# Branch rows converted by thirds of tokens as soon as their readers are done, branch projection steps given out by stage

## What is computed

```python
h = _rmsnorm(x, norm_in_w)
u = h @ w_in                       # z | x,B,C | dt | q,k,v x 3 | z_att | q_mem | z_mem | merge gates
y_ssd, new_conv, new_ssm = _ssd_branch(z_ssd, xbc, dt_raw, ...)      # conv, chunked scan, gated norm
y_att = o_att * silu(z_att);  y_mem = mem_attn(q_mem, mem_kv) * silu(z_mem)
merged = gates[0] * (y_ssd @ w_br_ssd) + gates[1] * (y_att @ w_br_att) + gates[2] * (y_mem @ w_br_mem)
y = _rmsnorm(x + merged @ w_out, norm_f_w)
```

## Time and profile before

| | us |
|---|---|
| median of 3 runs | 2108.25 (2104.48 to 2114.3) |
| the profiled execution | 2112.42 |
| its span on the core | 2110.6 |
| PE busy | 1979.0 (94%) |
| DVE, ACT, POOL busy | 985.8, 765.1, 242.0 |
| mean granted clock of TensorE | 0.965 of full |

### The profile page before, as it was taken

One profiled execution on the slowest core, in us unless ns is written; L12 is line 12 of the kernel. 1 busy time (PEld: TensorE's weight loads), 2 busy tenths in 40 slices (PEclk: granted clock), 3 DMA queues, 4 the chain that ended last, 5 costly groups with the idle time before them and its releaser, 6 DMA issues.

```text
span 2110.6 us, 34859 instructions
## 1 busy us (share of the span) xinstructions
PE 1979.0 (94%) x14301; PEld 1892.0 (90%) x14301; DVE 985.8 (47%) x1941; ACT 765.1 (36%) x1642; POOL 242.0 (11%) x358
## 2 busy tenths in 40 slices
PE   5999999999989999999999899999999669969997
PEld 5899999999989999999999889669999659969997
DVE  5303676535465354443337684013555455454523
ACT  5223444323353333332655223115556532133202
POOL 1000111100001010112212100001211111100000
PEclk9999999999999999999999999998999879989999
DMA  6311332311112121212256784764545635554422
GB/s 216 92 42 52 93 93 83 93 46 40 49 33 65 41 67 39 87 44 90 86 170 198 237 260 141 268 228 134 169 153 161 216 88 179 175 173 140 143 84 104
DMA packets 171742, 257.18 MB, mean 122 GB/s; under 512 B 20229, under 2 KB 115269, under 8 KB 171557
## 3 DMA queue, kind: packets, MB, share of 16 engines
q1 hardware_dynamic: 149328, 187.97, 28.4%
q0 software_dynamic: 22256, 66.98, 9.4%
HBM read 188.13 MB, written 66.76 MB: 121 GB/s over the span
## 4 chain that ended last, share of the span: by engine, by line
PE 85%; DVE 5%; ACT 4%; DMA 3%; issue 2%; SPq 0%; POOL 0%; DVEq 0%; ACTq 0%; POOLq 0%
PE bank L2296 21%; PE bank L2297 21%; PE bank L2298 21%; PE bank L2496 3%; PE bank L2469 2%; PE bank L2452 2%; PE bank L2711 2%; PE bank L2600 1%; PE bank L2430 1%; DVE w_lo L1762 1%; PE bank L2755 1%; PE bank L2533 1%; DMA sums<-sum_T 1%; PE bank L2395 1%; PE bank L2394 1%
## 5 line engine op out<-in xcount | busy, mean ns | idle before, releaser
L2296 PE MATMUL bank<-w_hi,hT_hi 128*128 128x256 f32 (+1 forms) x1848 | 536.9, 291 | 0.2 <-issue 0.2
L2297 PE MATMUL bank<-w_lo,hT_hi 128*128 128x256 f32 (+1 forms) x1848 | 524.6, 284 | 0.0
L2298 PE MATMUL bank<-w_hi,hT_lo 128*128 128x256 f32 (+1 forms) x1848 | 523.6, 283 | 0.0
L2296 PE MATMUL bank<-hT_hi,w_hi 128*128 128x352 f32 x1344 | 451.3, 336 | 6.3 <-DVE acc L2143 5.7
L2298 PE MATMUL bank<-hT_hi,w_lo 128*128 128x352 f32 x1344 | 439.1, 327 | 0.0
L2297 PE MATMUL bank<-hT_lo,w_hi 128*128 128x352 f32 x1344 | 438.8, 327 | 0.0
L2296 PEld LDWEIGHTS bank<-w_hi,hT_hi 128*128 128x128 f32 (+1 forms) x1848 | 349.8, 189 | 1.9 <-issue 0.5
L2298 PEld LDWEIGHTS bank<-w_hi,hT_lo 128*128 128x128 f32 (+1 forms) x1848 | 350.6, 190 | 0.6
L2297 PEld LDWEIGHTS bank<-w_lo,hT_hi 128*128 128x128 f32 (+1 forms) x1848 | 349.7, 189 | 1.3
L2296 PEld LDWEIGHTS bank<-hT_hi,w_hi 128*128 128x128 f32 x1344 | 257.8, 192 | 20.1 <-issue 8.6
L2297 PEld LDWEIGHTS bank<-hT_lo,w_hi 128*128 128x128 f32 x1344 | 258.8, 193 | 0.5
(11 more groups left out here) (423 smaller groups left out, 2934.6 us busy)
## 6 DMA issues: line engine op xcount, KB each, us to landing
w_raw<-in_w_in SPq DMA_DIRECT2D x96, 512.0 KB, 5.0
kvring<-in_cache_win_kv SPq DMA_DIRECT2D x98, 256.0 KB, 4.8
feat_T<-fstage POOLq DMA_DIRECT2D x40, 528.0 KB, 4.2
fstage<-feat_T SPq DMA_DIRECT2D x16, 528.0 KB, 4.2
xc<-feat_T SPq DMA_DIRECT2D x8, 1024.0 KB, 5.9
sums<-sum_T SPq DMA_DIRECT2D x32, 256.0 KB, 4.5
o_rows<-obuf POOLq DMA_DIRECT2D x48, 132.0 KB, 2.0
mo<-o_rows SPq DMA_DIRECT2D x24, 264.0 KB, 3.3
```

The costliest lines, as they stand in the source:

```text
L2296: pe.matmul(out, xh(k), wh(k), start=(k == 0), stop=False)
L2297: pe.matmul(out, xh(k), wl(k), start=False, stop=False)
L2298: ins = pe.matmul(out, xl(k), wh(k), start=False, stop=(k == nk - 1))
```

## The change

What it does, in the order of the kernel:
- Rows are no longer converted whole. Item g = 0 to 8 of `ya` and `yb` is third g // 3 of the tokens of rows 0 to 2, 3 to 5 or 6 and 7 (`YA_ROWS`): one load of 3 (2) runs of 352, one instruction on ACT, one on DVE. The loads have steps of their own, `yal` as before and `ybl` new.
- The last gate chunk's groups are dealt so that both readers of the first third come first, and `ya` 0 to 5 run between the gate groups, each as soon as its third has been read (`gates_read`). `ya` 6 to 8 follow the last gate group; ("p1", 52, 0, 0, 0) stands among them.
- `p1` groups wait for their third and branch alone (`s_yal` of 2 to 8).
- The scan's last steps are dealt in stages: 18 `p1` groups over the last ten groups of the prompt's scan, 4 over the next six, 10 over the 26 sample groups, 4 over the last five; 12 follow. Before it was one for each.
- `yb` overwrites the memory of `ya` (`hT`) by thirds behind the last `p1` groups that read it; `p2`'s result takes the memory that `yb` had. `yb` has a fourth buffer, `acc0`. `normf`, `osq` lie elsewhere.
- ("split", n) and ("low", n) keep their place at the end of their chunk; of the last gate chunk and of the last `p1` chunk they stand where the lists below show them.

```diff
+YA_ROWS = (slice(0, 3), slice(3, 6), slice(6, 8))
+YA_SLOT = (0, 1, 2, 0, 1, 2, 0, 1, 0)
+YB_SLOT = (0, 1, 2, 0, 3, 1, 2, 0, 3)
+P1_SCAN, P1_STATE, P1_SAMPLE, P1_LAST = 18, 4, 10, 4
...
-    n_gate, n_ya = 31, 4
-    core[n_gate - 3] += [("yal", k) for k in range(3)]
-    for i in range(n_ya):
-        core[n_gate + i] += [("yal", k) for k in ((3, 4), (5, 6), (7,), ())[i]]
-        core[n_gate + i] += [("ya", 2 * i), ("ya", 2 * i + 1)]
-    sched += spread(core[:n_gate], gate_steps(len(fill_src)))
-    for x in core[n_gate:n_gate + n_ya]:
-        sched += x
+    n_gate = 5 * (NB - 2) + 1
...
+    f00, f01, f02, f10, f11, f12 = [x[:1] for x in steps[-6:]]
+    steps[-6:] = [f00, f10, f01, f02, f11, f12 + [("split", last_gate)]]
+    sched += spread(core[:n_gate], steps)
...
-        steps.append([("split", n)])
-    sched += spread(core[n_gate + n_ya:], steps)
+        if i < 3:
+            steps[-1].append(("split", n))
+    parts = [(core[n_gate:n_gate + 1], 0), (core[n_gate + 1:n_gate + 11], P1_SCAN), (core[n_gate + 11:n_gate + 17], P1_STATE)]
+    parts += [(core[n_gate + 17:n_gate + 43], P1_SAMPLE), (core[n_gate + 43:], P1_LAST)]
+    done = 0
+    for groups, k in parts:
+        sched += spread(groups, steps[done:done + k])
+        done += k
+    sched += [("ssd", NB, 6)] + [("ybl", g) for g in range(3)]
+    for step in steps[done:-6]:
+        sched += step
+    b00, b01, b02, b10, b11, b12 = steps[-6:]
+    sched += b00 + [("yb", 0), ("ybl", 3), ("ybl", 4)] + b01 + b10 + [("yb", 1), ("ybl", 5), ("yb", 2), ("ybl", 6)]
+    sched += b02 + [("yb", 3), ("ybl", 7)] + b11 + [("yb", 4), ("ybl", 8), ("yb", 5), ("yb", 6)] + b12 + [("yb", 7), ("yb", 8), ("split", n)]
+    g = last_gate
+    behind(("ssd", NB - 4, 4), 0, [("yal", k) for k in range(3)])
+    behind(("feat", g, 1, 0), 0, [("ya", 0)])
+    behind(("ssd", NB - 4, 6), 0, [("ya", 1), ("yal", 3)])
+    behind(("ssd", NB - 3, 4), 0, [("ya", 2), ("yal", 4), ("yal", 5)])
+    behind(("feat", g, 1, 1), 0, [("ya", 3), ("ya", 4)])
+    behind(("feat", g, 1, 2), 0, [("yal", 6), ("ya", 5)])
+    behind(("ssd", NB - 2, 1), 0, [("p1g", 0, 0), ("yal", 7), ("ya", 6), ("p1g", 0, 1)])
+    behind(("ssd", NB - 2, 2), 0, [("ya", 7), ("yal", 8)])
+    behind(("p1", g + 1, 0, 0, 0), 0, [("ya", 8), ("low", g)])
...
                 elif s[0] == "ya":
-                    k = s[1]
-                    if k == 0:
-                        act.wait_ge(s_pj, n_act_proj)
-                    act.wait_ge(s_kv[k % 3], kv_loads(k % 3) + 16 * (k // 3 + 1))
-                    act.activation(yAh[:, k, :], ya_slot(k), ACT.Copy).then_inc(s_yah, 1)
+                    g = s[1]
+                    act.wait_ge(s_pj, gates_read[g // 3])
+                    act.wait_ge(s_kv[YA_SLOT[g]], kv_loads(YA_SLOT[g]) + ya_loads(YA_SLOT[g], g + 1))
+                    act.activation(ya_part(yAh, g), ya_slot(g), ACT.Copy).then_inc(s_yah, 1)
...
-                    if s[0] == "p1" and u == n_act_proj:
-                        pe.wait_ge(s_yal, KT8)
-                    if s[0] == "p2" and s[2:] == (0, 0) and chunks[n][1] == 0:
-                        pe.wait_ge(s_yal, KT8 + KT8)
+                    if s[0] == "p1" and u < n_act_proj + 6:
+                        pe.wait_ge(s_yal, 3 * s[4] + 2 + s[3])
+                    if s[0] == "p2" and chunks[n][1] + s[2] == 0:
+                        pe.wait_ge(s_yal, N_YA + 3 * s[3] + 3)
```

More of the change, by code:

```diff
@@ L975, in snew, with ya_slot, ya_part, ya_loads @@
             return (Lflat[:, D:2 * D] if b % 2 == 0 else yo[:, :]).rearrange("p (i n) -> p i n", i=8)
-        def ya_slot(k):
-            return (yraw, acc1, acc0)[k % 3][:, :]
+        def ya_slot(g):
+            rows = YA_ROWS[g % 3]
+            return (yraw, acc1, acc0)[YA_SLOT[g]][:, 0:THIRD * (rows.stop - rows.start)].rearrange("p (k n) -> p k n", n=THIRD)
+        def ya_part(buf, g):
+            j = g // 3
+            return buf[:, YA_ROWS[g % 3], THIRD * j:THIRD * j + THIRD]
+        def ya_loads(at, g):
+            return 16 * sum(YA_SLOT[x] == at for x in range(g))
+        def ya_last(at, g):
+            return 1 + max(x for x in range(g) if YA_SLOT[x] == at)
+        gates_read = [1 + max(u for x, u in proj.items() if x[0] == "feat" and x[3] == j) for j in range(3)]
         def acc_of(ft):
@@ L991, in build_program, with yb_slot, yb_sem, yb_landed @@
             gate_no["p2", ft] = n_sig
-        def yb_slot(k):
-            return (yraw2, gate2, acc2)[k % 3][:, :]
+        def yb_slot(g):
+            rows = YA_ROWS[g % 3]
+            return (yraw2, gate2, acc2, acc0)[YB_SLOT[g]][:, 0:THIRD * (rows.stop - rows.start)].rearrange("p (k n) -> p k n", n=THIRD)
+        def yb_sem(at):
+            return s_kv[(0, 1, 2, 5)[at]]
+        def yb_landed(g):
+            at = YB_SLOT[g]
+            x = (0, 1, 2, 5)[at]
+            return yb_sem(at), kv_loads(x) + (ya_loads(at, N_YA) if at < 3 else 0) + 16 * sum(YB_SLOT[i] == at for i in range(g + 1))
+        def yb_done(at, upto):
+            return N_YA + 1 + max(i for i in range(upto) if YB_SLOT[i] == at)
+        last_p1 = chunks.index(next(x for x in chunks if x[0] == "p1" and x[1] == KT8 - 2))
+        def rows_read(g):
+            return proj["p1", last_p1, 1, int(g % 3 > 0), g // 3] + 1
         def yst_of(c):
@@ L1182, in _ @@
                     load_gate(ft, br)
-                elif s[0] == "yb":
-                    k = s[1]
-                    if k == 0:
+                elif s[0] == "ybl":
+                    g = s[1]
+                    at, j, rows = YB_SLOT[g], g // 3, YA_ROWS[g % 3]
+                    if g == 0:
                         last_free(sp)
```

84 lines of the change are left out of this document (46 added, 38 removed).

## The result

The changed kernel took 2124.72 us (median of 6 runs, 2119.67 to 2128.77) against 2108.42 us beside it: a ratio of 1.0079, 95% interval 1.0060 to 1.0097. It is slower by 16 us, outside the range given. Its profiled execution took 2119.67 us for a span of 2117.8, 7.2 us above the span of before; the same kernel, run again later, took 2117.40 us (10 runs, ratio 1.0041, 1.0022 to 1.0060), and that profiled execution had a span of 2122.8. I use both. Neither profile is of a middle execution: the first is of the fastest of its six (2119.67 us), the second of the slowest of its ten (2124.54), and the profile of before is of an execution of 2112.42 us, 4 us above the median of its set and 5 to 6 above those of the later ones. Executions of over 3000 us (one of e7_ask_fill22, one of e12_fill22, and one of before in each of two sets) are left out of all medians.

What follows compares the result with a forecast made beforehand. The prediction took PE's idle time, from order on ACT, DVE and SP, as the bound; its terms went from 55.5 to 54.6 us, 1 us less, giving 2107 us (own range 2098 to 2116; 8 in 10 within 2092 to 2120).

Steps and rivals of the forecast that it cites:

- What bounds the kernel now: Opening step, 1660.3 to 1899.3 us: PE's work is unchanged, so only its idle time, 55.5 us, is summed.
- Rival (b): TensorE's clock: if the 14 us freed at 1700 us leave it fast, some 8 us more come back, 2099 us; chance 0.12.
- Rival (c): Slower: weights asked for behind the conversions land as late as 12.6 us, 11.5 us more, 2118 us; chance 0.18.
- Rival (a): Transfers land near their floor, 10.5 us less, 2096 us; chance 0.20.
- up to the last gate: Conversions ahead of the weight split and chunk 5's state on DVE: PE's idle time 0 to about 1 us.
- products of chunk 6: PE's wait before scan chunk 6's masked decay products, for chunk 53's late weights: 12.4 to 12.5 us.
- state of chunk 6: PE's wait before the second half of chunk 6's state, no conversion left ahead on DVE: 16.9 + 0.9 to 3.8 us.
- chunk 7: Scan chunk 7: chunk 52's split steps now stand ahead of its state, and a third group awaits a bank: 6.4 to 11.9 us.
- sample tokens: Sample steps: fewer groups between them (1.8 to 3.5 us) and chunk 53's weight split (5 us): 1.8 to 8.5 us.
- end: Last projections and p2: waits for banks 4.0, split 2.6, gate 4.5, conversions 1.3, p2 3.9 us; in all 17.1 to 16.9.
- sign of being right: Waits before Lm over 10 us, chunk 6's state near 4, chunk 7's near 10, sample part about 5; PE stops in p2.
- three signs of being wrong: Chunk 7's state wait below 6 us; idle time over 60 us; a p1 eviction waiting long for its gate.

Runs made afterwards that it cites:

- e7_ask_fill22: Changed kernel with weights of chunks 53 to 57 asked for early and projection groups dealt 10, 2, 22, 2; 2105.78 us, ratio to before 0.9981.
- e12_fill22: Changed kernel, conversions and requests as they are, with projection groups dealt 10, 2, 22, 2 (22 among the sample steps); 2106.26 us, ratio to before 0.9999.
- e9: Kernel before with only the dealing by stage, 10 projection groups and one split over the 26 groups of sample steps; 2115.43 us, ratio 1.0041.
- e4: Changed kernel with one gate row asked for ahead of the first three reads of merged rows; 2112.74 us, ratio to before 1.0034.
- e1: Changed kernel with weights of chunks 53 to 57 asked for right behind the low part of the chunk before; 2104.14 us, ratio to before 0.9996.
- e3: Changed kernel with split and low of chunk 52 behind the second part of scan chunk 7, not ahead; 2125.43 us, ratio to before 1.0094.
- e11: Kernel before with weights of chunks 53 to 57 asked for right behind the low part of the chunk before; 2105.91 us, ratio 1.0004.
- e10_combined: Changed kernel with early weights, groups dealt 12, 4, 16, 4, and one gate row ahead of the first merged rows; 2100.02 us, ratio to before 0.9969.

## Why the prediction was wrong

**The step that failed** is the one under "What bounds the kernel now": "the work of PE is the same before and after ... The sum is one of idle time." The work is the same, with 14301 matmuls in both; its clock is not. The sum has no term for it. The sample part's term went over "fewer groups now lie between the sample steps" and charged only the cover that they gave (1.8 us made 3.5). What those groups also did was to hold the clock; their absence costs 7 us in one profile of the changed kernel and 12 in the other, 9 in e9, and that comes back in e12. The forecast of 2107 us was 18 us low against the first set of runs and 10 against the second; in their profiles the idle sum is 2.7 and 1.2 us above the forecast, and the clock takes 7 and 12 us more than before.

**Rival (b)** named the clock but with one sign: freed time gives clock back, "against it, the new waits of 10 and 5 us slow it elsewhere". The loss needed no waits (e9). Nor did clock come back at chunk 6: from 1600 to 1750 us PE lost 8.7 us to it before and 10.3 and 9.2 in the two profiles of the changed kernel. The rows read for it were the mean of the whole stretch, 0.84, and one window at a wait. In the same 239 us the changed kernel has

```profile
1660.30:1899.30 239.00, 187.41 (x1130) 178.43 (x1129) 111.95 (x207) 61.38 (x110) 24.78 (x25) 0.81 0.46 147
```

with PE busy for 4 us more and the clock at 0.81. A row for the sample part alone, and the count of projection groups in it, were what the prediction lacked.

**Rival (c)**, 2118 us, is near the result by its number, and its mechanism did not happen. It needed landings of 12 us. On SP and ACT of the changed kernel:

```profile
1722.76 0.53 SPq L1173 DMA_DIRECT2D w_raw<-in_w_br_mem  x1
```

```profile
1729.46 1.91 ACT L1507 ACTIVATE w_hi<-w_raw 128x2048 fp32r<-128x2048 f32 x1 [14.13 <-DMA w_raw<-in_w_br_mem]
```

the weights of chunk 54 landed 6.7 us after the second request; 7.9 and 7.6 us for chunks 53 and 55. **Rival (a)**, landings at the floor of 4.8 us, did not happen either. The forecast had 7 us for chunk 54, with an estimate of 6.1 beside it. The reads of y rows in runs of 1408 bytes, for which no row stood, landed in 3.0 to 6.9 us from 1635 us on, whole rows before, three of them sent for at once, in 3.3 to 9.9.

The steps of the sum, with the two profiles of the changed kernel:

| term | forecast | measured | read as |
|---|---|---|---|
| up to the last gate | 1 | 0, 0 | no wait of 0.4 us or more |
| products of chunk 6 | 12.5 | 13.9, 13.7 | cause right: ACT's split waited for w_raw until 1669.8 us (1671.5 forecast). The prediction's own steps add up to 12.8 |
| state of chunk 6 | 3.8 | 3.7, 3.7 | right |
| chunk 7 | 11.9 | 13.5, 12.8 | cause right: `w_lo` at 1731.5 us just ahead of `yo`; the third group's bank 0.6, not 1.6 |
| sample tokens | 8.5 | 9.8, 10.2 | split 4.6 and 5.0, as said; the first steps 5.2, not 3.5 |
| end | 16.9 | 16.4, 15.4 | banks 4.2 (4.0 forecast), gate 4.6 (e4 confirms its cause), split 1.4, not 2.6; conversions 0, not 1.3; `p2` 5.7, 4.7, not 3.9 |
| sum | 54.6 | 57.3, 55.8 | |
| clock, busy time | 0 | +7, +12 | missing |

So all that the last part of the prediction named as a sign of being right was seen, and none of its three signs of being wrong; it lacked a sign for the clock. That the range ended at 2120 follows from the same gap: its upper bound was that of landings alone, and the clock entered only the lower one, as a gain.

The sentence that the gain at chunk 6 "is what the change is good for" holds in another way than meant. The gain there was real, 13 us of idle time, and was paid back at chunk 7 (7 us more than before) and in the sample part (8 us more), in large part by splits whose weights came late; with the weights asked for early (e1) the time is 13 to 21 us below the changed kernel's, still no more than equal to before.

## What to carry to other kernels

In this kernel the work that fills the gaps of a stage of small matmuls does two things: it covers waits, and it keeps TensorE's clock up. Before moving such work, read the granted clock of that stage by itself and not only PE's idle time, and keep a term for the clock in the sum, with both signs. And a stage that waits for a split of weights was cured where the weights are asked for (e1), not where the split stands: moving the split alone moved the wait one step on (e3). That holds only if nothing else ends the wait at about the same time; on the kernel before the same request gained nothing (e11).

## What was not expected of the hardware

The granted clock fell to 0.50 (1.2 GHz) in stretches in which PE had no wait at all: in e9 with PE busy for 82.73 of 83.46 us. The Trainium skill (TensorE: Matmul & The Clock Gate, Why this matters for your kernels) names idle gaps of PE as what brings the clock down; these runs show a loss without one, which followed the share of projection matmuls (352 columns) among sample matmuls of 4 and 128 columns. What it is in the sample matmuls was not tried: their few columns, the 32 rows that some of them use, that a part of them are transposes, or the weight loads between them.

The same program's loss varies: 15.2 and 20.7 us in two profiles, and 2112 to 2129 us in 16 executions, where before's 25 beside e1 to e4 lie from 2099 to 2115. Why the first set of the changed kernel's runs was slower by 7 us than the second, with before nearly equal in both (2108.4 and 2106.8), stays open; the mean granted clock differs (0.959 and 0.962), its cause was not found, and a difference between chips is not excluded. e10_combined's profile shows 7 us less gain in span than its idle time and its loss in the sample part would give; from 1600 to 1750 us, in windows of 5 us, its PE lost 13.7 us of busy time to the clock and that of before 8.7, which is most of it. What lowers the clock there was not tried.
